# Global attention of an encoder layer: the maxima product moved ahead of the weighing and a step further ahead, its maxima placed by four transfers, and one of eight probability steps summed by TensorE

## What is computed

```python
q = axial_rope(rmsnorm(q, gq), row, col)       # 8 heads, 2048 x 64
k = axial_rope(rmsnorm(k, gk), row, col)       # 2 heads, 2048 x 64
def one_block(qblk):
    s = jnp.einsum('bkgqd,bksd->bkgqs', qblk, k).astype(jnp.float32) * scale
    p = jax.nn.softmax(s, axis=-1).astype(v.dtype)
    return jnp.einsum('bkgqs,bksd->bkgqd', p, v)
```

## Time and profile before

| | us |
|---|---|
| median of 3 runs | 3029.72 |
| lowest and highest | 3029.05, 3031.0 |
| the profiled execution | 3032.3 |
| its span | 3030.7 |
| granted share of TensorE's clock over the span | 0.973 |

### The profile page before, as it was taken

How to read it: one execution, slowest core, us unless ns; L and a number is a source line. 1 busy time by engine, 2 the same in 40 slices (tenths; PEclk the granted TensorE clock), 3 DMA queues, 4 the chain that set the end, 5 groups by cost and what they waited for, 6 DMA issues and landing times. The chain is left out here.

```text
span 3030.7 us, 38875 instructions
## 1 busy us (share of the span) xinstructions
PE 2827.5 (93%) x12978; PEld 2318.1 (76%) x12978; DVE 1659.6 (55%) x2193; ACT 1329.4 (44%) x1882; POOL 910.1 (30%) x683
## 2 busy tenths in 40 slices
PE   7999499999999969979969999999999999999998
PEld 5888377777777738958858888888888888888887
DVE  5666388888888838855534432354224542254322
ACT  3222177777777738953323322244223432233221
POOL 1221189999999945532200000000001000010000
PEclk9999699999999979989979999999999999999999
DMA  5333611111111022348873343343434343343432
GB/s 174 107 107 98 159 25 32 30 29 34 27 34 29 18 78 79 83 139 206 235 215 98 97 147 90 110 134 97 151 90 134 109 125 118 93 151 97 122 94 83
DMA packets 473643, 308.96 MB, mean 102 GB/s; under 512 B 62451, under 2 KB 440579, under 8 KB 473148
## 3 DMA queue, kind: packets, MB, share of 16 engines
q1 hardware_dynamic: 443484, 274.46, 32.2%
q0 software_dynamic: 6496, 19.42, 2.0%
q10 hardware_dynamic: 23552, 13.64, 1.5%
HBM read 236.79 MB, written 66.40 MB: 100 GB/s over the span
## 5 line engine op out<-in xcount | busy, mean ns | idle before, releaser
L1686 DVE TENSOR_TENSOR f_w_lo<-f_w_raw,f_w_hi 128x1024 fp32r<-128x1024 f32 x256 | 313.8, 1226 | 864.3 <-ACT f_w_hi L1638 864.1
L1638 ACT ACTIVATE f_w_hi<-f_w_raw 128x1024 fp32r<-128x1024 f32 x256 | 271.4, 1060 | 980.4 <-PE f_down L122 553.1
L626 POOL TENSOR_TENSOR p_sum<-p_sum,p_hi 128x1024 f32<-128x1024 f32 x192 | 458.9, 2390 | 33.1 <-issue 25.1
L120 PE MATMUL f_up<-f_h,f_w_hi 128*128 128x512 f32 x1024 | 400.9, 391 | 19.7 <-DMA f_h<-h_split 19.7
L120 PE MATMUL f_down<-f_act_hi,f_w_hi 128*128 128x512 f32 x1024 | 401.2, 392 | 0.0
L122 PE MATMUL f_up<-f_h,f_w_lo 128*128 128x512 f32 x1024 | 399.8, 390 | 0.0
L121 PE MATMUL f_up<-f_h,f_w_hi 128*128 128x512 f32 x1024 | 399.8, 390 | 0.0
L122 PE MATMUL f_down<-f_act_hi,f_w_lo 128*128 128x512 f32 x1024 | 398.8, 389 | 0.0
L121 PE MATMUL f_down<-f_act_lo,f_w_hi 128*128 128x512 f32 x1024 | 398.3, 389 | 0.0
L679 DVE TENSOR_REDUCE part_max<-m_ps 128x1 f32<-128x1024 f32 x251 | 306.8, 1222 | 116.9 <-PE m_ps L724 116.9
L1614 POOL TENSOR_TENSOR f_rstd<-f_var,f_half 128x4 f32<-128x4 f32 x4 | 5.1, 1285 | 1186.3 <-DVE f_var L1706 1186.3
(11 more groups left out here) (202 smaller groups left out, 4841.3 us busy)
## 6 DMA issues: line engine op xcount, KB each, us to landing
f_w_raw<-in_w_ffn_up SPq DMA_DIRECT2D x128, 512.0 KB, 4.1
f_w_raw<-in_w_ffn_down SPq DMA_DIRECT2D x128, 512.0 KB, 3.8
f_h<-h_split SPq DMA_DIRECT2D x32, 512.0 KB, 5.7
x_in<-in_x SPq DMA_DIRECT2D x16, 512.0 KB, 4.2
q_split<-q_out ACTq DMA_DIRECT2D x16, 512.0 KB, 3.3
q_turned<-w_raw SPq DMA_DIRECT2D x16, 512.0 KB, 3.4
q_all<-q_turned SPq DMA_DIRECT2D x32, 256.0 KB, 3.3
wq_in<-q_split SPq DMA_DIRECT2D x32, 256.0 KB, 2.8
```

Source lines behind the costliest of these rows:

```text
L120: nc.tensor.matmul(out, stat_hi, mov_hi, start=first, stop=False)
L626: nc.gpsimd.tensor_tensor(p_sum[:, s], first, p_hi[:, (UNITS * n + u) % SLOTS].bitcast(F32), ALU.add).then_inc(added, 1)
L1638: nc.scalar.activation(w_hi[:, s], w_raw[:, s], ACT.Copy).then_inc(w_hi_made, 1)
L1686: nc.vector.tensor_tensor(w_lo[:, s], w_raw[:, s], w_hi[:, s].bitcast(F32), ALU.subtract).then_inc(w_lo_made, 1)
```

## The change

In `max_products` the queries are taken in order (`t * P:(t + 1) * P`), so `neg_max[p, t]` belongs to query 128t + p, and `place_max` issues four DMAs, one for each t, of 128 elements of 4 bytes. `EARLY` becomes 3: the last pair of the next block comes at step 4. On TensorE the maxima product stands between `scores` and `weigh`. VectorE's order is the same but for the pair numbers. GpSimd leaves out the addition of step 7 (`BY_ADDS` = 7), and TensorE adds that step's column sums with two products of the new tile `ones_low`, which put them into row 64 of `ob_ps`.

```diff
-    EARLY = 2
-    ADDS = UNITS
+    EARLY = 3
+    BY_ADDS = UNITS - 1
+    ADDS = BY_ADDS
...
+        ones_low = sb("g_ones_low", [P, 2 * HD], F32R)
...
             def place_max(n):
                 sp.wait_ge(max_ready, n + 1)
-                sp.dma_start(q_max[HD:HD + 1, n % QS].bitcast(F32).rearrange("o (p t) -> o p t", t=QT), neg_max[:, n % 2].bitcast(F32)).then_inc(max_placed[n % 2], 16)
+                for t in range(QT):
+                    row = q_max[HD:HD + 1, n % QS, t * P:(t + 1) * P].bitcast(F32)
+                    sp.dma_start(row.unsqueeze(2), neg_max[:, n % 2, t:t + 1].bitcast(F32)).then_inc(max_placed[n % 2], 16)
...
-                for u in range(1, UNITS):
+                for u in range(1, BY_ADDS):
                     pool.drain()
...
-                if at >= SLOTS:
-                    before = at - SLOTS
+                before = at - SLOTS
+                if at >= SLOTS and before % UNITS < BY_ADDS:
                     act.wait_ge(added, ADDS * (before // UNITS) + max(before % UNITS, 1))
...
-                    at_least(dve, max_placed[n % 2], 16 * (n // 2))
+                    at_least(dve, max_placed[n % 2], 16 * QT * (n // 2))
...
-                    last = nc.tensor.matmul(bank[:, e], q_all[:, n % QS, t::QT],
+                    last = nc.tensor.matmul(bank[:, e], q_all[:, n % QS, t * P:(t + 1) * P],
...
-                    pe.wait_ge(max_placed[n % 2], 16 * (n // 2 + 1))
+                    pe.wait_ge(max_placed[n % 2], 16 * QT * (n // 2 + 1))
...
+                for e in range(2 if u >= BY_ADDS else 0):
+                    last = nc.tensor.matmul(ob_ps[:], ones_low[:], p_hi[:, slot, e * QB:(e + 1) * QB], start=False, stop=False)
                 last.then_inc(high_used, 1)
...
                     scores(n, u)
-                    if at >= LAG:
-                        weigh((at - LAG) // UNITS, (at - LAG) % UNITS)
                     ahead, m = pair_of(n, u)
                     if ahead < TOTAL:
                         max_products(ahead, m)
+                    if at >= LAG:
+                        weigh((at - LAG) // UNITS, (at - LAG) % UNITS)
```

More of the change, by code:

```diff
@@ L606, in _ @@
             pool.drain()
-            nc.gpsimd.memset(ones_high[:, ONE_HIGH:], 1.0).then_inc(filled, 1)
+            nc.gpsimd.memset(ones_high[:, ONE_HIGH:], 1.0)
+            nc.gpsimd.memset(ones_low[:].bitcast(F32), 0.0)
+            pool.drain()
+            nc.gpsimd.memset(ones_low[:, ONE_LOW:ONE_HIGH].bitcast(F32), 1.0).then_inc(filled, 1)
             def combine(n):
```

## The result

| | before | changed | ratio |
|---|---|---|---|
| median | 3029.39 us (21 runs, 3028.02 to 3033.54) | 3034.19 us (21 runs, 3032.19 to 3047.9) | 1.0017, 95% interval 1.0011 to 1.0024 |

That is a small slowing, and inside the 0.2% that counts as no change. The profiled execution of the changed kernel, though, is the longest of its 21: 3047.9 us, span 3046.3 us.

What follows compares the result with a forecast made beforehand. GpSimd, without slack in its 22.01 us block, was taken to bound the kernel before. Thirty gaps of 22.25 us (+6.8 us) and the end (-3.5 us) gave +3.3 us: 3033 us, range a little below 3019 to a little above 3042.

Steps and rivals of the forecast that it cites:

- The loop: From step 1's scores through p_hi, GpSimd's adds, o_sum, store, four placings and step 0 to next step 1: 22.24 us.
- 0.64 us between issues: On SyncE's queue behind the store: spacing of the four placings, so three more issues add 1.92 us to a block.
- The last landing: The last of the four placings lands 2.0 us after its issue; TensorE starts step 0 some 0.1 us later.
- The sum: Whole global-attention stage: the gaps between copies of oa_ps and the stage's end together give +3.3 us.
- Thirty gaps: Between copies of oa_ps, one per block: 22.25 us each, 667.0 us in all against 660.2, +6.8 us.
- the last gap: Before the last block's copy of oa_ps: 0.47 us shorter, since the last block has no maxima product.
- The end: GpSimd's chain in the last block: earlier first add -1.2, one add less -2.55, wait for p_hi +0.3; together -3.5 us.
- The start: Ahead of the first block: one more maxima product and reduction, four issues for one; between -1 and +0.5 us, taken as 0.
- TensorE's floor: TensorE's products in one block, with the two new ones and the total: 20.0 us.
- The held negation: VectorE's negation of the maxima, in the middle of GpSimd's add 4: held 1 to 2 us, none seen in the time.
- Rivals 3 and 4: 3: placing not binding, held negation sets block, 21.0 us, 2996 us; 4: TensorE's floor, 20.0 us, 2966; together 0.08.
- Rival 1 and 2: 1: same loop, issues 0.48 us apart, 3019 us, chance 0.20; 2: dearer issues (0.74) or landings, 3042 to 3051 us, 0.22.

Runs made afterwards that it cites:

- the shifted one: The changed kernel with 84 repeated waits on TensorE ahead of the loop over the blocks (41 more instructions); median 3036.39 us, profiled execution 3033.87 us.
- the one with the late total: The changed kernel with the negation as a reduction and the two products of `total` moved from behind step 4 to behind step 7; 3034.77 us, ratio 1.0011.
- the second trace: The changed kernel run once more, unchanged; profiled execution 3047.55 us, ratio of the medians to the kernel before 1.0048.

## Why the prediction came out

**The loop and its terms.** Right, each within 0.03 us (above). The choice that mattered was 0.64 us between issues, taken from the same line on the same path, against 0.48 from small DMAs elsewhere: the trace has 0.64. The last landing was not delayed by the three ahead of it (2.0 us, as one alone). What had only been argued, that the way through the store and the four issues binds, the turned order of SyncE showed (22.2 to 21.2 us).

**The sum.** Thirty gaps +6.8 us forecast. Twenty-nine blocks of 22.2 us and a last gap of 23.1 make 666.9 us, +6.7, but by two errors that cancel: each block is 0.05 us shorter than forecast, and the last gap, for which I took 0.47 us off, is 0.9 us longer than the others. That is no accident of one trace: TensorE idles 2.0 to 2.4 us ahead of the last block, the clock falls behind it, and the last gap is 23.1 to 23.3 us in both traces of the changed kernel and in those of the shifted one, of the one with all adds on GpSimd and of the one with the late total. The end -3.5, measured -3.4. The start, given 0, measured -1.6 (-0.7 in the second trace). That makes +1.7 us where the sum said +3.3; the shortest executions differ by 4.2 us (3032.19 and 3028.02), the medians by 4.8. No trace shows where an execution of median length has the other 3 us, so that the median came within 1.5 us of the forecast is in part luck: slow issues and falls of the clock that the sum does not have filled what it had put too high.

**Order, third step, reading in order.** The first two were given nothing, and the kernel with them alone differs by 0.25 us from before. Reading in order was given nothing too, because the strided load "was already beside other products". That holds for the order before. Directly behind the scores it fails at two steps of eight: 0.29 us in a block of 20.26 us, close to TensorE's floor. In the changed kernel step 0 waits anyway, and it is covered.

**The held negation.** Forecast 1 to 2 us and covered; measured 1.6 us in most blocks. Covered it is, in the loop. But it does something that I had not thought of: it splits TensorE's idle time. I also forecast TensorE idle for over 1 us ahead of step 0; in undisturbed blocks it is 0.84 us, the rest lies at step 6, behind the held p_lo.

**Rivals 3 and 4.** Neither came true, but each has its kernel: placings out of the way give 21.2 us for my 21.0; the negation free as well gives 20.26 us for my floor of 20.0. Rival 1 and 2 hung on the price of an issue alone.

**What the prediction missed.** Two costs of waiting in the loop have no term in the sum: a DMA issue that takes 1.2 to 1.9 us beside an instruction packet, and the lower clock behind some of TensorE's idle stretches. Before, no placing was over 0.70 us, and between the first copy and the last the clock did not fall; nothing in the rows pointed to either. They gave the profiled execution 15 us, which puts it 6 us above the 3042 us of the range's upper side.

## What to carry to other kernels

When one transfer becomes several on a queue, ask whether its issue stands in the loop that sets the time, and behind what: here three more issues of 0.64 us made a block of 22.2 us of one of 21.5, and moving them ahead of one store gave 1%. Removing a stall off the bound can cost time if it joins idle pieces of TensorE, so look at the granted clock behind each wait that grows. Then compare parts alone and together: the sum alone was worth 11 us, the order alone nothing, and the four placings alone cost 7.

## What the runs showed of the hardware

- A negation of 128x4 elements as a multiplication by -1 is held to the end of GpSimd's running add (up to 1.90 us); as a reduction over one element it takes 0.157 us in 32 of 32 (156 to 160 ns), 31 of them beside a running GpSimd instruction.
- An issue of a placing, a small DMA between two tiles, takes 0.60 us right behind another issue and 0.49 to 0.51 us where the queue stood still before it (the placings ahead of the store); four in a row behind the store take 2.53 us. With a 16 KB packet on the instruction queue that begins up to 0.16 us behind its start it took 1.3 to 2.0 us in nine of ten cases of the first trace and in ten of ten with one placing, and 0.59 us in the one left. The issue of one row of denominators, 0.25 us, with such packets beside it, was not longer.
- Behind 1.7 us of idle TensorE the granted clock fell to 0.5 (1.2 GHz) for 3.4 us in 16 of 28 cases of one kernel; behind 1.4 us in none of 25 of another; behind 1.2 us in none of the steady blocks of a third. In the changed kernel it fell behind 4 of 11 idle pieces of 1.57 to 2.05 us, and one of 2.05 us brought no fall. Up to each fall it had been 1.00 (2.4 GHz).
- A weight load of 128x128 4-byte elements takes 0.31 us with a stride of four and 0.19 us in order.
